# A shorter early projection, late projections in halves spread over the gather stage, and an output matrix streamed for two tiles

## The reference, cut to what matters

```python
for x, cache in ((x_prompt, None), (x_sample, caches)):
    q_sb, k_sb, v_sb, q_sw, k_sw, v_sw = split(rms_norm(x) @ w_in)    # 1024 -> 2304 columns
    o_sb = stick_breaking(q_sb, k_sb, v_sb)           # 8 heads, over all earlier keys
    o_sw = sink_window_attention(q_sw, k_sw, v_sw)    # 8 heads, a window of 128 keys
    h = x + concat(rms_norm(o_sb), rms_norm(o_sw)) @ w_out
    q = rms_norm(h) @ w_peer_q                        # 8 routing heads
    ids, gate = product_key_top16(q, keys_1, keys_2)  # 16 of 16384 experts a head
    y = rms_norm(h + sum(gate * gelu(u[ids] . rms_norm(h)) * v[ids]))
```

## Time and profile before

| | us |
|---|---|
| median of 3 runs | 3419.69 |
| lowest, highest | 3415.66, 3427.44 |
| the profiled execution's own time | 3431.02 |
| its span | 3429.2 |

### The profile page before, as it was taken

One profiled execution on the slowest core, in us unless ns is written; L12 is line 12 of the kernel. 1 busy time (PEld: TensorE's weight loads), 2 busy tenths in 40 slices (PEclk: granted clock), 3 DMA queues, 4 the chain that ended last, 5 costly groups with the idle time before them and its releaser, 6 DMA issues.

```text
span 3429.2 us, 38100 instructions
## 1 busy us (share of the span) xinstructions
PE 2596.8 (76%) x10640; PEld 1186.2 (35%) x10640; DVE 2219.7 (65%) x5631; ACT 1386.9 (40%) x3222; POOL 1624.0 (47%) x1634
## 2 busy tenths in 40 slices
PE   7979886787768776877687767877787777777664
PEld 4545432243223322432243323432343234322221
DVE  2012765578667766777677766676777776675775
ACT  2011254255226532653265435642665344542322
POOL 0100344544565555545555554555554555455453
PEclk9989998898889988998899888998999888878777
DMA  5543899998999999999999999999999999999887
GB/s 159 168 131 102 337 337 416 390 356 337 377 394 387 380 403 383 405 372 391 388 390 383 370 399 363 375 375 414 378 394 366 413 400 386 391 389 387 349 354 300
DMA packets 271317, 1216.28 MB, mean 355 GB/s; under 512 B 29809, under 2 KB 122273, under 8 KB 134913
## 3 DMA queue, kind: packets, MB, share of 16 engines
q0 software_dynamic: 154560, 1113.51, 81.8%
q1 hardware_dynamic: 116544, 100.33, 9.2%
HBM read 1193.05 MB, written 20.79 MB: 354 GB/s over the span
## 4 chain that ended last, share of the span: by engine, by line
PE 36%; DMA 20%; DVE 12%; issue 7%; ACT 7%; POOL 6%; DVEq 3%; ACTq 2%; POOLq 0%; SPq 0%
DMA f_uv<-peer_uv,f_idx 18%; PE f_y_acc L1519 17%; PE f_q_ps L1458 6%; DVE f_uv L1033 5%; POOL f_uv L818 4%; PE f_z L1307 3%; PE f_z L1422 2%; PE f_y_acc L1401 2%; ACT f_diag L962 2%; ACT L956 2%; POOL f_gate_fold L806 2%; PE f_z L1288 2%; DMA f_work<-scratch_v_window 2%; PE f_z L1314 1%; PE f_o_sb L1333 1%
## 5 line engine op out<-in xcount | busy, mean ns | idle before, releaser
L818 POOL DMA_INDIRECT f_uv<-peer_uv,f_idx x1056 | 1279.1, 1211 | 1592.8 <-PE f_y_acc L1519 1296.2
L1033 DVE CUSTOM_DVE_ANT_0 f_uv<-f_uv,f_x_rep 128x1024 f32<-128x1024 f32 x1056 | 1301.4, 1236 | 747.8 <-DMA f_uv<-peer_uv,f_idx 740.5
L1519 PE MATMUL f_y_acc<-f_uv,f_diag 128*64 128x512 f32 x4224 | 1260.5, 720 | 600.2 <-ACT f_diag L962 573.9
L1519 PEld LDWEIGHTS f_y_acc<-f_uv,f_diag 128*64 128x64 f32 x4224 | 301.8, 154 | 1233.9 <-ACT f_diag L962 749.5
L956 ACT ACTIVATE f_act_hid<-f_hid 128x2 f32<-128x2 f32 x528 | 107.3, 203 | 1292.3 <-DVE f_hid L1033 1275.7
L1458 PE MATMUL f_q_ps<-r_w_q,f_xnT 128*128 128x256 f32 x1152 | 324.9, 436 | 82.5 <-DVE f_cut L1159 82.5
L962 ACT ACTIVATE f_diag<-f_gate_fold,f_act_hid 128x64 f32<-128x64 f32 x1056 | 310.3, 340 | 38.6 <-issue 1.7
L806 POOL TENSOR_TENSOR f_gate_fold<-r_fold,f_gates 128x128 f32<-128x128 f32 x528 | 317.3, 601 | 9.6
L1458 PEld LDWEIGHTS f_q_ps<-r_w_q,f_xnT 128*128 128x128 f32 x1152 | 242.1, 219 | 193.0 <-DVE f_cut L1159 98.5
L956 ACT ACT_TABLE_LOAD x195 | 250.2, 1283 | 3.4
L831 ACT ACT_TABLE_LOAD x119 | 152.7, 1283 | 202.4 <-PE f_z L1288 155.5
(11 more groups left out here) (175 smaller groups left out, 2638.9 us busy)
## 6 DMA issues: line engine op xcount, KB each, us to landing
f_uv<-peer_uv,f_idx POOLq DMA_INDIRECT x1056
f_work<-scratch_projT SPq DMA_DIRECT2D x86, 128.0 KB
w_cols<-w_in SPq DMA_DIRECT2D x18, 512.0 KB, 3.9
r_w_out<-w_in SPq DMA_DIRECT2D x18, 512.0 KB, 4.6
f_work<-out_sb_v_prompt SPq DMA_DIRECT2D x72, 128.0 KB
r_w_q<-w_peer_q SPq DMA_DIRECT2D x8, 1024.0 KB, 7.1
x_in<-x_prompt SPq DMA_DIRECT2D x8, 512.0 KB, 5.1
f_q_pad<-scratch_projT SPq DMA_DIRECT2D x64, 64.0 KB
```

What stands on the lines that cost most here:

```text
L818: pool.indirect_dma_start(uv[:, n % RING, :], None, io["peer_uv"], bass.IndirectOffsetOnAxis(ap=idx[:, t % 2, head, k:k + 1], axis=0),).th ...
L1033: nc.vector.tensor_tensor_reduce(row_u, row_u, x_rep[:, g % 2, :], 1.0, 0.0, ALU.mult, ALU.add, hid[:, n // 2 % 8, n % 2:n % 2 + 1]).then_ ...
L1519: last = nc.tensor.matmul(y_acc[i * GT:(i + 1) * GT, b * 512:(b + 1) * 512], diag[:, batch % 3, i, :], uv[:, n % RING, DM + b * 512:DM + ( ...
```

## The change

- **Early and late tiles.** `T_LATE` = 3: tiles 0 to 2 and the sample are early, tiles 3 to 7 late (640 columns). The early product is one group of eight products of 416 columns, evicted by one instruction, and the natural outputs take one PSUM bank.
- **36 units.** A late block is two units: 384 columns (tiles 3 to 5) and 256 (tiles 6 and 7), both from the same weights, which are loaded in two pieces of 256 KB into three buffers. The first three pieces are issued in phase one. Twelve units, every 7 slots, stand before the gathers, in turn in `y_acc` and `sel_ps`; 24 at slots 2, 9, 16, 23, 33, 40, 70, 77, 84, 91, 98, 112, 119 and eleven from 157 to 212.
- **Output matrix streamed.** The space is free only after slot 217, so `w_out` is loaded at slot 223. For tiles 1 and 2 (`STREAMED`) an eighth of it (512 KB) is loaded per step into one of two buffers, one of them the space of the final gain `g_final`, which is loaded anew after each of the two. Their eight steps stand two slots apart and not one (`stretch`, `PRODUCT_AT`, `TAIL_END_AT`).
- **Slots.** Routing of tile 0 starts at slot -25 and not -29; tile 1 has a head every 8 slots from 99 (before 9 from 95); tile 2 every 14 from 186 (before 15 from 179), tile 3 every 14 from 315 (before 15 from 307), tiles 4 to 7 every 14 (before 15). `select` now stands ahead of `queries` in a slot.

```diff
-EARLY = SEQ // 2
-ORDER = [0, 1, 2, 3, NT, 4, 5, 6, 7]
-N_EARLY = 5
+T_LATE = 3
+EARLY = T_LATE * P
+ORDER = [*range(T_LATE), NT, *range(T_LATE, NT)]
+N_EARLY = T_LATE + 1
 COLUMNS = SEQ - EARLY
+PIECES = ((0, 3 * P), (3 * P, COLUMNS))
+PIECE = 3 * P
+STREAMED = (1, 2)
...
+LATE_ORDER = [4, 5, 6, 7, 8, 9, 10, 11, 0, 17, 16, 1, 2, 3, 12, 13, 14, 15]
+
+def load_late(sync, io, r, p):
+    c, half = LATE_ORDER[p // 2], p % 2
+    src = io["w_in"].rearrange("(k p) n -> p k n", p=P)[:, 4 * half:4 * half + 4, c * P:(c + 1) * P]
+    sync.dma_start(r.w_late[:, p % 3, :, :], src).then_inc(r.s_w_late[p % 3], 16)
...
-                if i == N_EARLY - 1:
+                if i == 4:
...
-                    sp.dma_start(r.g_final[:], io["norm_final"].partition_broadcast(P)).then_inc(s_late_const, 16)
...
+            for p in range(3):
+                load_late(sp, io, r, p)
...
-                for a, b in ((0, EARLY), (EARLY, EARLY + TS)):
-                    for k in range(DK):
-                        last = nc.tensor.matmul(acc[c % 2][:, a:b], w[:, c % 2, k, :], xnT[:, k, a:b],
-                                                start=(k == 0), stop=(k == DK - 1))
+                for k in range(DK):
+                    last = nc.tensor.matmul(acc[c % 2][:, 0:EARLY + TS], w[:, c % 2, k, :], xnT[:, k, :],
+                                            start=(k == 0), stop=(k == DK - 1))
...
     if t == 0:
-        return 8 * head - 29
+        return 8 * head - 25
     if t == 1:
-        return 95 + 9 * head
-    return t * P - 77 + 15 * head if t < NT else t * P - 63 + 9 * head
+        return 99 + 8 * head
+    if t == 2:
+        return t * P - 70 + 14 * head
+    if t == 3:
+        return t * P - 69 + 14 * head
+    return t * P - 77 + 14 * head if t < NT else t * P - 63 + 9 * head
+
+def stretch(t):
+    return 7 if t in STREAMED else 0
 
 def tail_slot(t):
-    return route_slot(t, 0) - 28
+    return route_slot(t, 0) - 28 - stretch(t)
...
-LATE_SLOT = [FIRST_SLOT + 8 * (i + 1) for i in range(C_END)]
+LATE_SLOT = [*(FIRST_SLOT + 8 + 7 * i for i in range(12)), 2, 9, 16, 23, 33, 40, 70, 77, 84, 91, 98, 112, 119,
+             *(157 + 11 * i // 2 for i in range(11))]
+UNITS = [(c, half) for c in LATE_ORDER for half in range(2)]
...
+PRODUCT_AT = {tail_slot(t) + 9 + k * (2 if t in STREAMED else 1): (t, k) for t in range(NT + 1) for k in range(DK)}
...
+            def next_late(p):
+                i, half = divmod(p - 3, 2)
+                if half:
+                    hold(sync, S["late_mm"], 2 * i + 2)
+                else:
+                    hold(sync, S["late_w"], i + 1)
+                load_late(sync, io, r, p)
+
+            def stream_w_out(t, k):
+                if k >= 2:
+                    hold(sync, S["op_w"], STREAMED.index(t) * DK + k - 1)
+                elif k == 0:
+                    hold(sync, S["pvw"], 4 * t + 4)
+                elif t > STREAMED[0]:
+                    hold(sync, S["y_out"], t - 1)
+                sync.dma_start(w_stream[k % 2], io["w_out"][k * P:(k + 1) * P, :]).then_inc(S_WS[k % 2], 16)
+
+            def load_g_final(t):
+                hold(sync, S["op"], t + 1)
+                sync.dma_start(g_final[:], io["norm_final"].partition_broadcast(P)).then_inc(S["g_final"], 16)
...
+                if (t := TAIL_AT.get(n - 1)) in STREAMED:
+                    stream_w_out(t, 0)
+                    stream_w_out(t, 1)
+                if (at := PRODUCT_AT.get(n - 1)) and at[0] in STREAMED and at[1] + 2 < DK:
+                    stream_w_out(at[0], at[1] + 2)
...
+                if (u := LATE_AT.get(n - 7)) is not None and UNITS[u][0] in KEPT:
+                    store_late(u)
+                if (u := LATE_AT.get(n - 7)) is not None and u % 2 == 1:
+                    for p in range(u + 2, min(u + 4, len(UNITS))):
+                        next_late(p)
...
-                if n == LATE_SLOT[-1] + 9:
+                if n == LATE_SLOT[-1] + 11:
...
+                if t in STREAMED:
+                    pe.wait_ge(S_WS[k % 2], (STREAMED.index(t) * DK // 2 + k // 2 + 1) * 16)
+                    w = w_stream[k % 2]
...
+                if (at := ROUTE_AT.get(n - 16)):
+                    select(at[0] * PH + at[1], n)
                 for half in range(2):
                     if (at := ROUTE_AT.get(n - half)):
                         queries(at[0] * PH + at[1], half)
-                if (at := ROUTE_AT.get(n - 16)):
-                    select(at[0] * PH + at[1], n)
```

More of the change, by code:

```diff
@@ L443 @@
 FIRST_SLOT = step_slot(0, 0) - 8
-LATE_ORDER = NATURAL + [c for c in range(C_END) if c not in NATURAL]
-LATE_SLOT = [FIRST_SLOT + 8 * (i + 1) for i in range(C_END)]
-LATE_AT = {slot: i for i, slot in enumerate(LATE_SLOT)}
+LATE_SLOT = [*(FIRST_SLOT + 8 + 7 * i for i in range(12)), 2, 9, 16, 23, 33, 40, 70, 77, 84, 91, 98, 112, 119,
+             *(157 + 11 * i // 2 for i in range(11))]
+UNITS = [(c, half) for c in LATE_ORDER for half in range(2)]
+LATE_AT = {slot: u for u, slot in enumerate(LATE_SLOT)}
+LATE_NATURAL = [u for u, (c, half) in enumerate(UNITS) if c in NATURAL and (c != C_KVSW or half == 1)]
+BEFORE_GATHERS = sum(slot < 0 for slot in LATE_SLOT)
 GATHERS = (NT + 1) * P - 3 * TS
@@ L452 @@
 TAIL_AT = {tail_slot(t): t for t in range(NT + 1)}
+TAIL_END_AT = {tail_slot(t) + stretch(t): t for t in range(NT + 1)}
+PRODUCT_AT = {tail_slot(t) + 9 + k * (2 if t in STREAMED else 1): (t, k) for t in range(NT + 1) for k in range(DK)}
 ROUTE_AT = {route_slot(t, head): (t, head) for t in range(NT + 1) for head in range(PH)}
@@ L533, in fused_phase @@
         S_V = [sem(f"v{i}") for i in range(2)]
-        S_WL = [sem(f"w_late{i}") for i in range(2)]
+        S_WL = r.s_w_late
+        S_WS = [sem(f"w_stream{i}") for i in range(2)]
         S_LST = [sem(f"stage_late_stored{i}") for i in range(2)]
@@ new lines, in late_bank, with units_in, late_size, turn_bank @@
+        def late_bank(u):
+            return {"y_acc": y_acc[:, 0:512], "sel_ps": sel_ps[:], "o_sb": o_sb[:], "o_sw": o_sw[:]}[late_place(u)]
+        def units_in(place, before):
+            return [u for u in range(before) if late_place(u) == place]
+        def late_size(u):
+            a, b = PIECES[u % 2]
+            return b - a
+        def turn_bank(u):
+            return y_acc[:, 512:512 + late_size(u)] if u < BEFORE_GATHERS else o_sw[:, 0:late_size(u)]
+        def evicted(n):
+            return sum(slot + 6 < n for slot in LATE_SLOT)
@@ new lines, in natural_before, with stage_stores, nat_targets @@
+        def natural_before(n):
+            return sum(LATE_SLOT[u] + 8 < n for u in LATE_NATURAL)
+        def stage_stores(u):
+            return sum(UNITS[j][0] in KEPT for j in range(u % 2, u, 2))
+        def nat_targets(u):
+            c, half = UNITS[u]
+            a, b = PIECES[half]
+            if c == C_KVSW:
+                return [(flat(io, "swa_k_prompt"), b // P - a // P - 1)]
+            every = [(natural_rows(io, c, EARLY + a, b - a), None)]
+            return every + [(flat(io, "swa_v_prompt"), b // P - a // P - 1)] if c == C_END - 1 and half else every
@@ L606, in _, with nat_stores, all_nat_stores @@
+        def nat_stores(j):
+            return sum(len(nat_targets(LATE_NATURAL[i])) for i in range(j % 2, j, 2))
+        def all_nat_stores(s):
+            return sum(len(nat_targets(LATE_NATURAL[i])) for i in range(s, len(LATE_NATURAL), 2))
         @block.sync
@@ L728, in store_late_natural, with store_late @@
-            def store_late_natural(i):
-                hold(sync, S["late_nat"], i + 1)
-                for dst, only in nat_targets(i):
+            def next_late(p):
[5 more added lines that the diff above has]
+                load_late(sync, io, r, p)
+            def store_late(u):
+                c, half = UNITS[u]
+                a, b = PIECES[half]
+                hold(sync, S["late_ev"], u + 1)
+                sync.dma_start(io["projT"][c, :, EARLY + a:EARLY + b], r.stage_late[:, u % 2, 0:b - a]
+                               ).then_inc(S_LST[u % 2], 16)
```

246 lines of the change are left out of this document (127 added, 119 removed).

## The result

The changed kernel took 3451.35 us (median of 4 runs, 3438.66 to 3453.2), the kernel before 3420.36 (4 runs). The ratio is 1.0064, 95% interval 1.0042 to 1.0086: 22 us slower, where 70 us less were forecast. The profiled execution took 3438.7 us with a span of 3436.9, the lowest of the four.

What follows compares the result with a forecast made beforehand. TensorE was taken to bound everything before the first dot product, mostly DMA the gather stage after it. Front 97.5 us earlier less back part +27 gave 70.5 us less: 3349 us, range 3315 to 3400.

Steps and rivals of the forecast that it cites:

- The front: Everything before the first dot product: 97.5 us earlier in all, bounds 75 to 107.
- 57 + 5.5: Phase one's product, 57 us less from 5.59 us blocks, and entry into phase two, scores 5.5 us earlier.
- From scores to first dot product: Slots before the gathers: 17 and 12 us less in two windows, from fewer late products and transposes.
- The feared shortage of weights: Phase one: in eight blocks the next weights may come 0 to 1 us late, 0 to 8 us lost.
- Slots 0 to 47: First slots with gathers, 159 us before: 10 us less, bounds -20 to +3, with select ahead of queries.
- cost 0, if nothing waits in order: Slots 157 to 217: 50 us more product on TensorE fits within what the bytes already stretch, cost 0.
- Rival 1: Slots 157 to 217 run at TensorE's pace, the back part costs 75 us, time 3397; chance 0.20.
- Pitch 8: Tile 1's heads 8 slots apart and not 9: +5 us, range 0 to +15.
- The streams: w_out streamed for two tiles: waits of about 0.6 us in 14 steps, +4 us, bounds 0 to +25.
- The bytes' +33: Slots 48 to 255: 17 MB more behind the DMA cost 19 to 41 us, taken as +33.
- rival 1's clock: Smaller rival inside rival 1: TensorE's granted clock, 0.84 to 0.88 at about 75% busy, 1.00 at 95%.
- Pitch 14: Heads 14 slots apart for 15 in tiles 2 to 7: -5 us, bounds -18 to +10.

Runs made afterwards that it cites:

- e2: The changed kernel without 12 of its 16 streamed loads of w_out (output not the layer's): 1.0022 to the kernel before.
- e3: The changed kernel with w_out loaded in eight parts of 512 KB, 8 slots apart from slot 227: 1.0049 to the kernel before.
- e10: The changed kernel with tile 1's heads 9 slots apart and nothing else: 1.0013 to the kernel before.
- e7: e4 with select behind queries in a slot again, as before the change: 0.9974 to the kernel before.
- e1: The changed kernel with the piece for the second half of the next late block issued four slots earlier: 0.9993 to the kernel before.
- e4: The changed kernel with the edits of e1 and e3 together: 3408.6 us, 0.9951 to the kernel before.
- e6: e4 without 12 of the 16 streamed loads of w_out (output not the layer's): 3385.8 us, 0.9874 to the kernel before.
- e11: e5 without 12 of the 16 streamed loads of w_out (output not the layer's): 3363.8 us, 0.9818 to the kernel before.
- e8: e4 with 12 of the 16 streamed loads issued from ACT's queue and not SP's: 0.9959 to the kernel before.
- e5: e4 with tile 1's heads 9 slots apart in place of 8: 3386.7 us, 0.9881 to the kernel before.
- e12: e5 with heads 15 slots apart in tiles 4 to 7, as before the change: 0.9872 to the kernel before.

## Why the prediction was wrong, point by point

**The front was right.** Forecast 97.5 us earlier, measured 89.6. The first product came 5.4 us earlier (6 forecast). The way from it to the first scores shrank from 188.2 to 134.0 us, by 54.2 where 57 + 5.5 = 62.5 were forecast: most blocks take 5.75 us and not 5.59, the first took 8.5 us (10.6 before), one turn of a late tile waited 3.1 us for DVE, and the third block behind it took 7.3 us at a granted clock of 0.78. From scores to first dot product it was 139.0 and is 109.0 us, 30.0 less (29 forecast). The feared shortage of weights was 0.6 us.

**Slots 0 to 47 can't be called right or wrong**: 6 us less in this profile, 10 forecast. But the kernels that share the changed kernel's code up to slot 47 (e2, e3 and e10) take 154.0 to 158.7 us there, for 159.2 before, and e7 doesn't show that the order of select matters. In the 16 slots after, where the load of w_out used to be, 8 us went in the changed kernel and 7 to 10 in the others.

**The step that failed is "cost 0, if nothing waits in order"** in the part on TensorE in slots 157 to 217. The condition was written down and not worked out there. The prediction did work out the piece's lead for the slots before the gathers, where units are 7 slots apart: issued at slot + 7, used at slot + 10. Where units are 5.5 apart the same lines give use at slot + 8.5, 1.5 slots or some 4 us, and the landing is that under gathers, 16.6 us in the case shown, not the 3.9 us of the earlier trace rows. The runs show 62.8 us of such waits, and e1 removes them: 24 us, uncertain by 10, and 30 us in slots 176 to 223. Rival 1 had placed the loss in these slots and given it to TensorE's pace; the busy share of 69% and e1 say that it was a wait.

**w_out at slot 223 got no term of its own, and nobody asked what it stands in front of.** Four 1 MB loads are issued just as tile 3's first keys are needed, and those land behind them: 16.4 us of wait, 18 us in slots 224 to 255. In the time it is 14 us in e4 against e1 and 5 in e3 by itself, each uncertain by some 10.

**Pitch 8 was mis-sized**: +5 forecast, 24 us measured at e4, 17 on the changed kernel. The prediction took tile 0's pace, 26.5 us a head, plus little. Slots 112 to 175 of e4 are 3.80 us each, a head 30.4 us; at pitch 9 they are 3.38, 30.5 us a head. A head costs the same time either way here, so each slot between two heads is a slot with nearly no price. Why a head takes 30 us here and 26.5 in tile 0 isn't shown. That a head took 28.9 us in these slots before (9 x 3.21) stood in the earlier trace rows and would have given 8 x 28.9 + 8 x 2.6 = 252 in place of 231: the right size.

**The streams**: +4 for waits, and their 9.4 MB were most of the +33 for bytes. Taking two thirds of these bytes out (12 of the 16 loads) gives 14, 26 and 22 us (e2, e6, e11); 15 are the bytes at the saturated rate, and that is within the uncertainty of each. Two thirds of the waits went in e8 without a gain, so a rest, if there is one, stays open. The landing taken, 8.2 us, was right as a median (8.0 in e4), but its spread, 3.6 to 23.6 us, goes far past the upper bound of 10.5: TensorE waited 13.7 us for streamed weights in the changed kernel and 27.7 in e4, where 8 were forecast. The fit that the prediction takes from the Trainium skill (DMA: Bandwidth & Descriptors, Anatomy of one DMA) is given there for DMAs issued by GpSimd, while these loads are issued by SP.

**The bytes' +33** can't be seen in the changed kernel, whose DMA share in slots 112 to 255 fell; it appears once the waits are gone. In e5 slots 176 to 255 have a share of 1.01 at 404 GB/s, and take 12.4 us more than before:

```profile
833.40:1066.70 233.30, 186.90 (x774) 87.18 (x772) 153.07 (x373) 95.16 (x222) 128.08 (x126) 0.93 1.01 404
```

The same line answers rival 1's clock: 42 us of late product lie in these slots (50 in slots 157 to 217), TensorE is busy 80%, granted 0.93 for 0.88, and it isn't the bound.

**Pitch 14**: -5 forecast, e12 finds nothing beyond the uncertainty in tiles 4 to 7, inside the bounds.

**In sum**, the overrun between forecast and result is 92 us (70.5 + 22). Pieces (24 us), w_out's place (14), pitch (24) and 12 streamed loads (22) are 84 us, and e11, without them, is at 0.9818 where the forecast was 0.979. That is no agreement: the forecast held 5 us for the pitch and, for those 12 loads, some 3 for waits and 15 for bytes. Beyond what was forecast the four cost some 61 us, and the front brought 8 less. Some 23 us of the overrun stay open. Part may lie in slots 256 on, where the profile of e5 is 16 us above the one of the kernel before and 5 less were forecast; with one profile of each kernel, and 10 to 17 us of uncertainty on each difference, the size is not settled. The first three costs were needless: e5 has the whole change in it but for the pitch of tile 1, and runs 1.2% faster than the kernel before. Earlier starts for tile 1's heads at pitch 9 were not tried.

## What to carry to other kernels

Here the work taken off the bound of one stage came back nearly in full (89.6 us of 97.5); what decided was the stage that received it. For every load in an order written by hand, work out its lead (slots from issue to use, at the tightest spacing that the order has anywhere, times the slot's time) and set it against the landing in that stage, not in an idle one. And for a big load ask what is issued behind it: its own deadline may be far off while the small load behind it is due now.

## What the runs showed of the hardware

A load's landing among the gathers has a wide spread: the 16 streamed loads of 512 KB took 3.6 to 23.6 us in e4, median 8.0. With the issue of 12 of them moved to a second engine's queue TensorE's waits for them fell by some two thirds (27.7 to 8.6 us) while the time stayed within 0.1%: a wait that disappears from the profile needn't have been a cost.

While TensorE waited for one late load, the DMA share stayed at 1.02; it fell to 0.00 only after the wait, when the buffers that the waiting products should have released were missing.
